# Key projections in a two-layer decoder trunk: the two halves of the memory tokens as one 512-column moving operand, with the two partial sums added by VectorE

## The chip, the cores and the metric

The kernel runs on one core of a Trainium2 chip. The metric is the device time of one execution in microseconds (us). The kernel before takes 1613.98 us, the median of 3 runs (1613.49 to 1614.69).

The engines are named as the profile names them: PE is TensorE's matmul, PEld its weight load, DVE is VectorE, ACT is ScalarE, POOL is GpSimd, SP is SyncE. They run side by side, each through its own list in a fixed order, and wait for each other on semaphores.

## The reference, cut to what matters

Two layers work on 512 tokens of 1024 features. Each has a token mixer, a cross-attention into 256 memory tokens, and an MLP. The change touches the key projection `k = mem @ wk` of the cross-attention, once in each layer:

```python
def _mem_cross_attn(h, mem, wq, wk, wv, wo):
    q = (h @ wq).reshape(bsz, seqlen, XA_HEADS, XA_HEAD_DIM)
    k = (mem @ wk).reshape(bsz, mem.shape[1], XA_HEADS, XA_HEAD_DIM)   # 256 x 1024
    v = (mem @ wv).reshape(bsz, mem.shape[1], XA_HEADS, XA_HEAD_DIM)
    s = jnp.einsum('bthd,bmhd->bhtm', q, k) * (XA_HEAD_DIM ** -0.5)
    pr = jax.nn.softmax(s, axis=-1)
    o = jnp.einsum('bhtm,bmhd->bthd', pr, v).reshape(bsz, seqlen, D_MODEL)
    return o @ wo

for i in range(DEPTH):                      # DEPTH = 2
    ...                                     # h = LN(alpha*h + mixer(h))
    h = _layer_norm(DN_ALPHA * h + _mem_cross_attn(h, mem, ...), ...)
    ffn = jnp.square(jax.nn.relu(h @ ffn_w1[i])) @ ffn_w2[i]
    h = _layer_norm(DN_ALPHA * h + ffn, ...)
```

## The kernel before

**Split numbers.** Every float32 operand of a large matmul is split into a high half (`_hi`, rounded by ACT to the matmul's float32r type) and a low half (`_lo`, what is left, by DVE). A product is the sum of three matmuls: weight high by input high, weight high by input low, weight low by input high.

**Weights** come as a stream of chunks of 128x1024 through three slots. For each chunk SP issues the load of `w_raw`, ACT writes `w_hi` (`split`, L1574), DVE writes `w_lo` (`split`, L2138), and PE reads both. A chunk's slot is free for the chunk three places further on when PE has finished with it (semaphore `chunk_done`). `split(n)` means: all chunks before number n. Keys, values and queries of a layer are 8 chunks each (k_0 to k_7, v_0 to v_7, q_0 to q_7).

**Keys.** `feature_major` (its matmuls are L778) makes one tile of 128 key features by 256 memory tokens from each chunk k_i. For each of the 8 blocks of the contraction it issues the weight's high half against the memory's high half and then against its low half (256 columns each), and after them the weight's low half against the memory's high half, 8 matmuls: 24 matmuls of 256 columns a tile, all summed into columns 0 to 255 of one of the 8 PSUM banks. The memory's halves lie in `aux_hi` and `aux_lo`. ACT then copies the sum from the bank into `k_hi` (`copy_hi`, L1587), and DVE subtracts that from the bank into `k_lo` (L2151).

**What follows on PE.** `to_features` transposes the hidden rows (24 matmuls, L1367) into six banks, which are those of k_0 to k_5; then v_0 is multiplied (L852) into the banks of k_6 and k_7. Each bank is taken when `k_out` says that DVE has written the `k_lo` of the tile in it.

**What sets the order.** Each engine's list is written out by hand. In `attention`, ACT and DVE go through i = 0 to 7, and each i is: `chunk(k_i)`, that is the split of the chunk three places ahead (for i under 3 that is already done in the layer norm before, so that the first one split here is k_5, ahead of tile 3) and then the wait for chunk k_i; then this tile's `k_hi` or `k_lo`. Before tile 0, DVE's list holds the row statistics and the scaling of that layer norm. POOL does nothing in this stretch.

Of the kernel before, what the change touches and what calls it, by code (L numbers as in the profile page):

```python
# [15 lines left out]
F32R = mybir.dt.float32r  # L16
# [212 lines left out]
def build(nc, x_tok, x_feat, mem_feat, weights, vectors, lora, lru_w, ln_rows, out):  # L229
    with ExitStack() as ctx:  # L230
# [3 lines left out]
        def sb(name, shape, dt=F32, at=None):  # L234

            size = 4
            for n in shape[1:]:
                size *= n
            if at is None:
                at = place["at"]  # L240
                place["at"] = at + (size + 31) // 32 * 32
            return nc.alloc_sbuf_tensor_at(name, shape, dt, offset=at)
# [9 lines left out]
        aux_at = place["at"]  # L252
        aux_hi = sb("aux_hi", [P, 8, T], F32R)
        aux_lo = sb("aux_lo", [P, 8, T], F32R)
        b_at = place["at"]
        k_hi = sb("k_hi", [P, 8, MEM], F32R)
        k_lo = sb("k_lo", [P, 8, MEM], F32R)
# [89 lines left out]
        a_hi = sb("a_hi", [P, 2, 4, 256], F32R, at=aux_at + 16384)  # L347
        a_lo = sb("a_lo", [P, 2, 4, 256], F32R, at=aux_at + 24576)
        s3 = sb("s3", [P, 4, 256], at=stage_at + 4 * 2048)

        def a_block(t, k):

# [10 lines left out]
        def hi_slot(c):  # L363
            return w_hi[:, SLOT[c]] if SLOT[c] < W_SLOTS else x_hi[:, SLOT[c] - W_SLOTS]
# [98 lines left out]
        def S(name):  # L463
            if name not in sems:
                sems[name] = ctx.enter_context(nc.semaphore(name))
            return sems[name]
# [5 lines left out]
        def bank(stg, i):  # L472
            return ps[BANK[stg, i]]

        def of(stg, suffix, n):


            return S(FAMILY[stg] + suffix), BEFORE[stg] + n
# [275 lines left out]
        def _(pe):  # L754
# [601 lines left out]
            def to_features(l, which, first=0, last=KD):  # L1356

                n = 3 * l + which
                for t in range(NT):
# [5 lines left out]
                    for k in range(first, last):  # L1365
                        o = take(f"lnt{l}_{which}", k) if t == 0 else bank(f"lnt{l}_{which}", k)
                        ins = pe.transpose(o[:, t * P:t * P + P], h[:, t, k * P:k * P + P], ident[:])  # L1367
                        if t == NT - 1:
                            ins.then_inc(S("lnt_mm"), 1)

            def attention(l):
                pe.wait_ge(S("mem_split"), l + 1)
                memv = [a[:].rearrange("p a t -> p (a t)")[:, 0:8 * MEM].rearrange("p (a t) -> p a t", a=8)
                        for a in (aux_hi, aux_lo)]
                feature_major(f"k{l}", 8, memv[0], memv[1], MEM)
                to_features(l, 0, 0, 6)
                token_major(f"v{l}", 2, KD, memv[0], memv[1], between={4: lambda: to_features(l, 0, 6, 8)})
                def scores(hp, first, last):
# [162 lines left out]
        def _(act):  # L1541
# [17 lines left out]
            def split(upto):  # L1559

                while n_split[0] < min(upto, N_CHUNKS):
                    c = n_split[0]
                    if c not in DOWN_OF:
                        act.wait_ge(landed[RAW[c]], 16 * (NTH_PLAIN[c] // W_SLOTS + 1))
                    else:
                        d, i = DOWN_OF[c]
                        name = PRODUCTS[i // 2][1]
                        if name in B_BLOCK:
                            act.wait_ge(*block_in(name, d))
                        else:  # L1570
                            act.wait_ge(S("t_sum"), 8 * d + 2 * T_ORDER.index(name) + i % 2 + 1)
                    if SLOT_PREV[c] is not None:
                        act.wait_ge(S("chunk_done"), SLOT_PREV[c] + 1)
                    act.activation(hi_slot(c), raw_chunk(c), ACT.Copy).then_inc(S("w_hi_done"), 1)  # L1574
                    n_split[0] += 1
# [10 lines left out]
            def copy_hi(stg, i, dst, n=T):  # L1586
                done(act.activation(dst, bank(stg, i)[:, 0:n], ACT.Copy), FAMILY[stg] + "_hi")  # L1587
# [225 lines left out]

            def memory(l):
                act.wait_ge(S("mem_in"), 16 * (l + 1))
                memv = aux_hi[:].rearrange("p a t -> p (a t)")[:, 0:8 * MEM]
                done(act.activation(memv, stage[:].rearrange("p a t -> p (a t)")[:, 0:8 * MEM], ACT.Copy), "mem_hi")

            def attention(l):
                ln_std(3 * l)  # L1820
                split(FIRST[f"k{l}"] + W_SLOTS)
                for i in range(8):
                    chunk(f"k{l}", i)
                    copy_hi(f"k{l}", i, k_hi[:, i], MEM)
                for half in range(2):
                    for i in range(4):
                        for k in range(4 * half + i + (half + i > 0), min(4 * half + i + 2, KD)):
# [282 lines left out]
        def _(dve):  # L2110
# [12 lines left out]
            def done(ins, name):  # L2123

                counts[name] = counts.get(name, 0) + 1
                ins.then_inc(S(name), 1)
                dve.wait_ge(S(name), counts[name])

            def f(ap):

                return ap.bitcast(F32)
# [9 lines left out]
            def chunk(stg, i):  # L2141
                c = FIRST[stg] + i
                split(c + W_SLOTS)
                dve.wait_ge(S("chunk_done"), c + 1)
# [5 lines left out]
            def tt(o, a, b_, op):  # L2150
                return dve.tensor_tensor(o, a, b_, op)  # L2151
# [376 lines left out]
            def memory(l):  # L2528
                dve.wait_ge(S("mem_hi"), l + 1)
                n8 = 8 * MEM  # L2530
                done(tt(aux_lo[:].rearrange("p a t -> p (a t)")[:, 0:n8], stage[:].rearrange("p a t -> p (a t)")[:, 0:n8],
                        f(aux_hi[:].rearrange("p a t -> p (a t)")[:, 0:n8]), SUB), "mem_split")

            def attention(l):
                split(FIRST[f"k{l}"] + W_SLOTS)
                for i in range(8):
                    chunk(f"k{l}", i)
                    dve.wait_ge(*of(f"k{l}", "_hi", i + 1))
                    done(tt(k_lo[:, i], bank(f"k{l}", i)[:, 0:MEM], f(k_hi[:, i]), SUB), "k_out")
                for half in range(2):  # L2540
                    for i in range(4):
                        for k in range(4 * half + i + (half + i > 0), min(4 * half + i + 2, KD)):
# [446 lines left out]
```

## Time and profile before

| | us |
|---|---|
| median of 3 runs | 1613.98 |
| the profiled execution: its time | 1614.45 |
| its span in the trace | 1612.4 |
| PE busy in it | 1566.9 (97%) |
| DVE busy | 1177.8 (73%) |
| ACT busy | 843.7 (52%) |
| granted TensorE clock, mean | 0.995 |

The span runs from the first to the last instruction in the trace; 2.05 us of the execution's time lie around it. Busy shares are averages over the whole program, and the busy time of PE is that of a pipeline (a matmul's row lasts longer than the distance to the next one), so that what a stretch is limited by is read from its own rows. Layer 1's attention is layer 0's over again, 802.06 us later.

### The profile page before, as it was taken

The numbers are of one execution on the slowest core, as the hardware profiler recorded it, in microseconds if no ns is written. First come the engines' busy times: TensorE is split into PE (matmuls) and PEld (weight loads), VectorE is DVE, ScalarE is ACT, GpSimd is POOL, SyncE is SP. The second block draws the span as 40 slices with busy tenths as digits, with TensorE's granted clock in tenths as the row PEclk, the third lists the DMA queues.
The fourth block names the chain that finished last, engine by engine and source line by source line (L and its number), as shares of the span: only waits on it lengthen the run. The fifth ranks groups of instructions, "written<-read, shape, count | busy, mean of one in ns | idle before, by whom it ended". The sixth has DMA issues, their size and how long they took to land.

```text
span 1612.4 us, 24422 instructions
## 1 busy us (share of the span) xinstructions
PE 1566.9 (97%) x9706; PEld 1303.1 (81%) x9706; DVE 1177.8 (73%) x1356; ACT 843.7 (52%) x1087; POOL 196.7 (12%) x189
## 2 busy tenths in 40 slices
PE   9999999999999999999899989999999999999996
PEld 8877888988878788888687876889887787888885
DVE  4569767664778868686998985756647788676768
ACT  4645643464355454545468855635553654545454
POOL 6111201001100000000026733200010000000001
PEclk9999999999999999999999999999999999999999
DMA  5222004442151505151042220244411605050501
GB/s 214 79 78 67 16 4 146 144 152 70 53 219 43 183 26 178 31 197 38 14 144 79 92 91 14 106 150 138 145 65 53 235 27 186 28 178 27 196 0 52
DMA packets 40784, 159.57 MB, mean 99 GB/s; under 512 B 4064, under 2 KB 4192, under 8 KB 39264
## 3 DMA queue, kind: packets, MB, share of 16 engines
q1 hardware_dynamic: 40384, 155.93, 28.6%
q10 hardware_dynamic: 288, 2.10, 0.3%
q8 instruction: 77, 1.26, 0.3%
q14 instruction: 35, 0.29, 0.1%
HBM read 153.81 MB, written 4.19 MB: 98 GB/s over the span
## 4 chain that ended last, share of the span: by engine, by line
PE 80%; DVE 13%; ACT 4%; issue 3%; POOL 0%; DVEq 0%; ACTq 0%; POOLq 0%
PE bank L778 41%; PE bank L1457 14%; PE bank L852 14%; DVE h L2151 2%; DVE sconv L2154 1%; PE bank L997 1%; PE bank L1012 1%; DVE h L2154 1%; DVE mix L2151 1%; DVE bank L2154 1%; DVE a_lo L2151 1%; DVE lnst L2651 1%; PE bank L1367 1%; DVE w_lo L2138 1%; PE bank L1091 0%
## 5 line engine op out<-in xcount | busy, mean ns | idle before, releaser
L778 PE MATMUL bank<-act_hi,w_hi 128*128 128x512 f32 x840 | 331.7, 396 | 6.0 <-DVE sconv L2154 5.0
L778 PE MATMUL bank<-act_lo,w_hi 128*128 128x512 f32 x840 | 327.4, 391 | 0.0
L2138 DVE TENSOR_TENSOR w_lo<-w_raw,w_hi 128x1024 fp32r<-128x1024 f32 x173 | 218.8, 1270 | 131.4 <-ACT w_hi L1574 128.2
L1574 ACT ACTIVATE w_hi<-w_raw 128x1024 fp32r<-128x1024 f32 x173 | 183.0, 1061 | 111.0 <-PE bank L852 78.2
L778 PE MATMUL bank<-act_hi,w_lo 128*128 128x512 f32 x840 | 212.0, 390 | 0.0
L778 PEld LDWEIGHTS bank<-act_hi,w_hi 128*128 128x128 f32 x840 | 158.6, 189 | 42.7 <-DVE sconv L2154 5.5
L778 PEld LDWEIGHTS bank<-act_lo,w_hi 128*128 128x128 f32 x840 | 158.6, 189 | 34.0 <-issue 1.2
L778 PEld LDWEIGHTS bank<-act_hi,w_lo 128*128 128x128 f32 x840 | 157.9, 188 | 33.0 <-DVE w_lo L2138 0.4
L702 POOL TENSOR_TENSOR cacc<-cacc,cprod 128x512 f32<-128x512 f32 x52 | 75.6, 1454 | 458.3 <-ACT cprod L1944 455.8
L1898 ACT ACTIVATE bank<-bank 128x512 f32<-128x512 f32 x64 | 37.2, 582 | 166.3 <-PE bank L778 166.3
L852 PE MATMUL bank<-w_hi,act_hi 128*128 128x512 f32 x288 | 112.6, 391 | 1.5 <-DVE act_lo L2151 1.5
L852 PE MATMUL bank<-w_hi,act_lo 128*128 128x512 f32 x288 | 112.1, 389 | 0.0
L1889 ACT ACTIVATE a_hi<-a_raw 128x1024 fp32r<-128x1024 f32 x48 | 51.0, 1062 | 67.9 <-PE bank L1457 62.8
L778 PE MATMUL bank<-act_hi,x_hi 128*128 128x512 f32 x208 | 81.5, 392 | 0.7 <-ACT act_hi L1801 0.6
L778 PE MATMUL bank<-act_lo,x_hi 128*128 128x512 f32 x208 | 80.8, 390 | 0.2
L1457 PE MATMUL bank<-w_hi,a_lo 128*128 128x512 f32 x264 | 73.0, 391 | 3.1 <-DVE a_lo L2151 3.0
L852 PE MATMUL bank<-w_lo,act_hi 128*128 128x512 f32 x288 | 74.7, 389 | 0.0
L1457 PE MATMUL bank<-w_hi,a_hi 128*128 128x512 f32 x264 | 72.5, 389 | 0.0
L1457 PE MATMUL bank<-w_lo,a_hi 128*128 128x512 f32 x264 | 71.3, 389 | 0.0
L2151 DVE TENSOR_TENSOR h<-h,bank 128x512 f32<-128x512 f32 x96 | 65.7, 684 | 2.0
L2138 DVE TENSOR_TENSOR w_lo<-b_raw,w_hi 128x1024 fp32r<-128x1024 f32 x46 | 55.4, 1223 | 16.1 <-ACT w_hi L1574 15.2
L852 PEld LDWEIGHTS bank<-w_hi,act_hi 128*128 128x128 f32 x288 | 54.1, 188 | 12.9 <-issue 1.6
(374 smaller groups left out, 3044.2 us busy)
## 6 DMA issues: line engine op xcount, KB each, us to landing
w_raw<-weights SPq DMA_DIRECT2D x199, 512.0 KB, 3.5
b_raw<-weights SPq DMA_DIRECT2D x32, 1024.0 KB, 4.9
gb<-ln_rows SPq DMA_DIRECT2D x6, 1024.0 KB, 8.2
stage<-x_feat SPq DMA_DIRECT2D x4, 512.0 KB, 6.0
h<-x_tok SPq DMA_DIRECT2D x1, 2048.0 KB, 7.9
stage<-mem_feat ACTq DMA_DIRECT2D x2, 1024.0 KB, 7.7
spill<-h SPq DMA_DIRECT2D x1, 2048.0 KB, 6.7
h<-spill SPq DMA_DIRECT2D x1, 2048.0 KB, 7.8
```

Of the source, the lines that this page charges most:

```text
L702: pool.tensor_tensor(cacc2[:, j % 2], cacc2[:, j % 2], cprod[:, added % 2], ALU.add)\
L778: return pe.matmul(banks[i][:, 0:n], w(c0 + i)[:, k * P:k * P + P], x[:, k, 0:n], start=first, stop=last)
L852: return pe.matmul(o[t][:, 0:HALF], x[:, slot[k], t * P:t * P + P], w(c0 + k // 2)[:, kk * HALF:kk * HALF + HALF], start=first, stop=last)
L997: last = each(lambda c, q, tok, feat, cf, ct: pe.matmul(compact(o, j, c, q, n), M_[b][tok, j, ct], halves(NBH[b][tok, j, ct], n, True), st ...
L1012: last = each(lambda c, q, tok, feat, cf, ct: pe.matmul(compact(o, j, c, q, n), left[tok, j, ct], halves(right[tok, j, ct], n, v < 5), sta ...
L1457: return pe.matmul(o[t][:], a[:, slot, k, t * P:t * P + P], w(c0 + k // 2)[:, k % 2 * HALF:k % 2 * HALF + HALF], start=(after is None and ...
L1574: act.activation(hi_slot(c), raw_chunk(c), ACT.Copy).then_inc(S("w_hi_done"), 1)
L1889: done(act.activation(a_hi[:, n % 2], A_OPERAND[name], ACT.Copy), "x_hi")
L1898: step(act.activation(o[:], o[:], ACT.Relu))
L2138: dve.tensor_tensor(lo_slot(c), raw_chunk(c), f(hi_slot(c)), ALU.subtract).then_inc(S("w_split"), 1)
L2151: return dve.tensor_tensor(o, a, b_, op)
L2154: return dve.scalar_tensor_tensor(out=o, in0=a, scalar=s, in1=b_, op0=op0, op1=op1)
```

## The change

The memory's halves lie side by side in one buffer, `mem_both`, in the place where `aux_hi` was. The new `keys` issues for each block one matmul of 512 columns, the weight's high half against both halves of the memory: columns 0 to 255 of the bank get the high part, columns 256 to 511 the low part. The weight's low half goes against the memory's high half as before, into columns 0 to 255. A tile is then 8 matmuls of 512 columns and 8 of 256.

The key is now the sum of the bank's two halves. DVE copies the right half into `k_raw` (a new buffer of two tiles), adds the left half, and raises `t_sum`. ACT, which read the bank, waits for `t_sum` and copies `k_raw` to `k_hi`. DVE then makes `k_lo` out of `k_raw` and `k_hi`. The other users of `t_sum` have their counts moved.

```diff
+        mem_both = sb("mem_both", [P, 2, 8, MEM], F32R, at=aux_at)
+        k_raw = sb("k_raw", [P, 2, MEM], at=stage_at + 4 * 2048)
...
+            def keys(l):
+                for i in range(8):
+                    c = FIRST[f"k{l}"] + i
+                    o = take(f"k{l}", i)
+                    pe.wait_ge(S("w_hi_done"), c + 1)
+                    for k in range(KD):
+                        pe.matmul(o[:], hi_slot(c)[:, k * P:k * P + P], mem_both[:, :, k], start=k == 0, stop=k == KD - 1,
+                                  skip_group_check=True)
+                    pe.wait_ge(S("w_split"), c + 1)
+                    for k in range(KD):
+                        last = pe.matmul(o[:, 0:MEM], lo_slot(c)[:, k * P:k * P + P], mem_both[:, 0, k], start=False,
+                                         stop=k == KD - 1, skip_group_check=True)
+                    last.then_inc(S("chunk_done"), 1)
...
-                feature_major(f"k{l}", 8, memv[0], memv[1], MEM)
+                keys(l)
...   (ACT)
                 for i in range(8):
                     chunk(f"k{l}", i)
-                    copy_hi(f"k{l}", i, k_hi[:, i], MEM)
+                    act.wait_ge(S("t_sum"), key_sum(l, i))
+                    done(act.activation(k_hi[:, i], k_raw[:, i % 2], ACT.Copy), "k_hi")
...   (DVE)
                 for i in range(8):
                     chunk(f"k{l}", i)
+                    step(dve.tensor_copy(k_raw[:, i % 2], bank(f"k{l}", i)[:, MEM:2 * MEM]))
+                    done(tt(k_raw[:, i % 2], k_raw[:, i % 2], bank(f"k{l}", i)[:, 0:MEM], ADD), "t_sum")
                     dve.wait_ge(*of(f"k{l}", "_hi", i + 1))
-                    done(tt(k_lo[:, i], bank(f"k{l}", i)[:, 0:MEM], f(k_hi[:, i]), SUB), "k_out")
+                    done(tt(k_lo[:, i], k_raw[:, i % 2], f(k_hi[:, i]), SUB), "k_out")
```

DVE's list at the start of layer 0's keys, before (bank4 to bank7 and bank0 hold tiles 0 to 4, the first row is the end of the layer norm; line numbers of the two kernels differ):

```order
L2468 TENSOR_SCALAR h_52<-h_52,lnmv_79,lnsd_80 128x1024 [waits dve_step]
L2151 TENSOR_TENSOR k_lo_58<-bank4,k_hi_57 128x256 [waits k_hi,chunk_done,ln_last]
L2151 TENSOR_TENSOR k_lo_58<-bank5,k_hi_57 128x256 [waits k_hi,chunk_done,k_out]
L2151 TENSOR_TENSOR k_lo_58<-bank6,k_hi_57 128x256 [waits k_hi,chunk_done,k_out]
L2138 TENSOR_TENSOR w_lo_51<-w_raw_49,w_hi_50 128x1024 [waits w_hi_done,k_out]
L2151 TENSOR_TENSOR k_lo_58<-bank7,k_hi_57 128x256 [waits k_hi,chunk_done]
L2138 TENSOR_TENSOR w_lo_51<-w_raw_49,w_hi_50 128x1024 [waits w_hi_done,k_out]
```

The same place now:

```order
L2489 TENSOR_SCALAR h_52<-h_52,lnmv_80,lnsd_81 128x1024 [waits dve_step]
L2559 COPY k_raw_103<-bank4 128x256 [waits chunk_done,ln_last]
L2172 TENSOR_TENSOR k_raw_103<-k_raw_103,bank4 128x256 [waits dve_step]
L2172 TENSOR_TENSOR k_lo_59<-k_raw_103,k_hi_58 128x256 [waits k_hi,t_sum]
L2559 COPY k_raw_103<-bank5 128x256 [waits chunk_done,k_out]
L2172 TENSOR_TENSOR k_raw_103<-k_raw_103,bank5 128x256 [waits dve_step]
L2172 TENSOR_TENSOR k_lo_59<-k_raw_103,k_hi_58 128x256 [waits k_hi,t_sum]
L2559 COPY k_raw_103<-bank6 128x256 [waits chunk_done,k_out]
L2172 TENSOR_TENSOR k_raw_103<-k_raw_103,bank6 128x256 [waits dve_step]
L2172 TENSOR_TENSOR k_lo_59<-k_raw_103,k_hi_58 128x256 [waits k_hi,t_sum]
L2159 TENSOR_TENSOR w_lo_51<-w_raw_49,w_hi_50 128x1024 [waits w_hi_done,k_out]
```

Two instructions stand ahead of each `k_lo`, and the `k_lo` stands between them and the next tile's.

ACT's list at the same place, before (the last `w_hi` of the layer norm, tiles 0 to 2, `w_hi` of k_5, tile 3, `w_hi` of k_6):

```order
L1574 ACTIVATE w_hi_50<-w_raw_49 128x1024 [waits chunk_done,w_landed1,ln_std]
L1587 ACTIVATE k_hi_57<-bank4 128x256 [waits chunk_done]
L1587 ACTIVATE k_hi_57<-bank5 128x256 [waits chunk_done,k_hi]
L1587 ACTIVATE k_hi_57<-bank6 128x256 [waits chunk_done,k_hi]
L1574 ACTIVATE w_hi_50<-w_raw_49 128x1024 [waits chunk_done,w_landed2,k_hi]
L1587 ACTIVATE k_hi_57<-bank7 128x256 [waits chunk_done]
L1574 ACTIVATE w_hi_50<-w_raw_49 128x1024 [waits chunk_done,w_landed0,k_hi]
```

And now:

```order
L1594 ACTIVATE w_hi_50<-w_raw_49 128x1024 [waits chunk_done,w_landed1,ln_std]
L1845 ACTIVATE k_hi_58<-k_raw_103 128x256 [waits t_sum,chunk_done]
L1845 ACTIVATE k_hi_58<-k_raw_103 128x256 [waits t_sum,chunk_done,k_hi] x2
L1594 ACTIVATE w_hi_50<-w_raw_49 128x1024 [waits chunk_done,w_landed2,k_hi]
L1845 ACTIVATE k_hi_58<-k_raw_103 128x256 [waits t_sum,chunk_done]
L1594 ACTIVATE w_hi_50<-w_raw_49 128x1024 [waits chunk_done,w_landed0,k_hi]
```

Nothing has moved; each `k_hi` has the wait for `t_sum`, and `w_hi` of the later chunks stands behind it as before.

## Rows read from the trace of the kernel before

**Rows 1.** The page, busy time, share of the span and instructions of each engine.
```profile
PE 1566.9 (97%) x9706; PEld 1303.1 (81%) x9706; DVE 1177.8 (73%) x1356; ACT 843.7 (52%) x1087; POOL 196.7 (12%) x189
```

**Rows 2.** The chain that ended last, in time: start us, us, what.
```profile
297.97 23.03 PE bank L778 x192
321.01 2.62 PE bank L1367 x24
323.63 5.47 PE bank L852 x24
...
1100.03 23.03 PE bank L778 x192
```

**Rows 3.** Timeline of PE, keys to first values: start us, us, engine, line, operation.
```profile
297.81 0.28 PE L778 MATMUL bank<-aux_hi,w_hi 128*128 128x256 f32 x1
...
300.68 0.28 PE L778 MATMUL bank<-aux_hi,w_hi 128*128 128x256 f32 x1
...
320.84 2.78 PE L1367 MATMUL bank<-ident,h 128*128 128x128 f32 x24
323.38 0.47 PE L852 MATMUL bank<-w_hi,aux_hi 128*128 128x512 f32 x1
...
326.21 0.39 PE L852 MATMUL bank<-w_hi,aux_hi 128*128 128x512 f32 x1
...
327.12 0.39 PE L852 MATMUL bank<-w_hi,aux_hi 128*128 128x512 f32 x1
```

**Rows 4.** Timeline of DVE over the keys of layer 0, idle before in brackets.
```profile
307.16 0.81 DVE L2468 TENSOR_SCALAR h<-h,lnmv,lnsd 128x1024 f32<-128x1024 f32 x1
308.01 1.34 DVE L2151 TENSOR_TENSOR k_lo<-bank,k_hi 128x256 fp32r<-128x256 f32 x3
309.38 1.23 DVE L2138 TENSOR_TENSOR w_lo<-w_raw,w_hi 128x1024 fp32r<-128x1024 f32 x1
310.53 0.42 DVE L2151 TENSOR_TENSOR k_lo<-bank,k_hi 128x256 fp32r<-128x256 f32 x1
...
312.89 0.42 DVE L2151 TENSOR_TENSOR k_lo<-bank,k_hi 128x256 fp32r<-128x256 f32 x1 [0.56 <-ACT k_hi L1587]
...
321.53 0.43 DVE L2151 TENSOR_TENSOR k_lo<-bank,k_hi 128x256 fp32r<-128x256 f32 x1 [0.57 <-ACT k_hi L1587]
```

**Rows 5.** Timeline of ACT over the keys of layer 0.
```profile
304.99 0.78 ACT L1587 ACTIVATE k_hi<-bank 128x256 fp32r<-128x256 f32 x2
...
307.12 1.06 ACT L1574 ACTIVATE w_hi<-w_raw 128x1024 fp32r<-128x1024 f32 x1
...
312.40 0.38 ACT L1587 ACTIVATE k_hi<-bank 128x256 fp32r<-128x256 f32 x1 [1.40 <-PE bank L778]
312.82 1.06 ACT L1574 ACTIVATE w_hi<-w_raw 128x1024 fp32r<-128x1024 f32 x1
```

**Rows 6.** Groups of one shape: busy us, mean ns of one | idle before.
```profile
L2468 DVE TENSOR_SCALAR h<-h,lnmv,lnsd 128x1024 f32<-128x1024 f32 x10 | 8.1, 814 | 0.4
L2151 DVE TENSOR_TENSOR k_lo<-bank,k_hi 128x256 fp32r<-128x256 f32 x16 | 6.8, 424 | 4.7 <-ACT k_hi L1587 4.5
L2151 DVE TENSOR_TENSOR v_lo<-bank,v_hi 128x512 fp32r<-128x512 f32 x8 | 5.5, 689 | 1.0 <-ACT v_hi L1587 0.8
L2803 DVE COPY stm<-bank 128x64 f32<-128x64 f32 x2 | 0.4, 224 | 0.1
L2060 ACT ACTIVATE act_hi<-p 128x512 fp32r<-128x512 f32 x8 | 5.1, 632 | 10.5 <-DVE p L2154 10.5
```

**Rows 7.** PE around its longest idle time in this trace.
```profile
932.44 0.80 PE L778 MATMUL bank<-act_hi,w_hi 128*128 128x512 f32 x1 [4.97 <-DVE sconv L2154]
...
936.02 0.40 PE L778 MATMUL bank<-act_hi,w_hi 128*128 128x512 f32 x1
```

**Rows 8.** PE by stretches: length, busy (instructions), granted clock, DMA share, GB/s.
```profile
807.00:808.00 1.00, 1.00 (x4) 0.50 0.72 115
930.00:935.00 5.00, 2.56 (x6) 0.50 0.25 91
```

More of the change, by code:

```diff
@@ L349, in build, with key_sum @@
         s3 = sb("s3", [P, 4, 256], at=stage_at + 4 * 2048)
+        k_raw = sb("k_raw", [P, 2, MEM], at=stage_at + 4 * 2048)
+        def key_sum(l, i):
+            return 8 * (QUARTERS + 1) * l + i + 1
         def a_block(t, k):
@@ L1369, in to_features @@
                             ins.then_inc(S("lnt_mm"), 1)
+            def keys(l):
[11 more added lines that the diff above has]
+                    last.then_inc(S("chunk_done"), 1)
             def attention(l):
                 pe.wait_ge(S("mem_split"), l + 1)
-                memv = [a[:].rearrange("p a t -> p (a t)")[:, 0:8 * MEM].rearrange("p (a t) -> p a t", a=8)
-                        for a in (aux_hi, aux_lo)]
-                feature_major(f"k{l}", 8, memv[0], memv[1], MEM)
+                memv = mem_both[:, 0], mem_both[:, 1]
+                keys(l)
                 to_features(l, 0, 0, 6)
@@ L1570, in split @@
                         else:
-                            act.wait_ge(S("t_sum"), 8 * d + 2 * T_ORDER.index(name) + i % 2 + 1)
+                            act.wait_ge(S("t_sum"), 8 * (d + d // QUARTERS + 1) + 2 * T_ORDER.index(name) + i % 2 + 1)
                     if SLOT_PREV[c] is not None:
@@ L1815, in memory @@
                 act.wait_ge(S("mem_in"), 16 * (l + 1))
-                memv = aux_hi[:].rearrange("p a t -> p (a t)")[:, 0:8 * MEM]
+                memv = mem_both[:, 0].rearrange("p a t -> p (a t)")
                 done(act.activation(memv, stage[:].rearrange("p a t -> p (a t)")[:, 0:8 * MEM], ACT.Copy), "mem_hi")
@@ L2530, in memory @@
                 n8 = 8 * MEM
-                done(tt(aux_lo[:].rearrange("p a t -> p (a t)")[:, 0:n8], stage[:].rearrange("p a t -> p (a t)")[:, 0:n8],
-                        f(aux_hi[:].rearrange("p a t -> p (a t)")[:, 0:n8]), SUB), "mem_split")
+                done(tt(mem_both[:, 1].rearrange("p a t -> p (a t)"), stage[:].rearrange("p a t -> p (a t)")[:, 0:n8],
+                        f(mem_both[:, 0].rearrange("p a t -> p (a t)")), SUB), "mem_split")
             def attention(l):
```

## The prediction

> **What bounds the kernel now.** I read the page first: PE is busy for 97% of the span [rows 1]. Then the chain that ended last, in time: through the keys of each layer it is PE alone, one piece of 23.03 us that ends in the transposes (L1367), and these in the first values (L852) [rows 2]. Then the timelines of this stretch. PE goes from tile to tile without a pause: k_0 begins at 297.81, k_1 at 300.68, so a tile of 24 matmuls takes 2.88 us, 0.120 us for each matmul of 256 columns; the eighth ends at 320.84, the transposes take 2.54 us, and v_0 begins at 323.38 [rows 3]. Layer 1 repeats this 802.06 us later [rows 2].
>
> The share of PE hides how close the other two engines are. Follow one round of theirs: ACT writes `k_hi` from 312.40 to 312.78, then at once `w_hi` of the chunk three places ahead, to 313.88 [rows 5]; DVE takes 0.11 us to see `k_hi` and writes `k_lo` [rows 4], then `w_lo`, whose successor can start 1.15 us after it (309.38 to 310.53) [rows 4]. From the end of a tile that is 0.04 + 0.38 + 0.04 + 1.06 + 0.10 + 1.15 = 2.77 us of a period of 2.88. So they have a tenth of a microsecond to spare per tile, and what keeps PE fed is that they run three chunks ahead. And they start late: DVE is in the layer norm's scaling until 307.97 [rows 4], ACT has its first `k_hi` at 304.99 [rows 5], while k_0 was finished at 300.7.
>
> **The change, part by part.**
>
> PE. Per block of the contraction two matmuls of 256 columns (2 x 0.120 us) become one of 512. The pace of those is in the values: four from 326.21 to 327.12, 0.227 us each [rows 3]. A pair gives back 0.240 - 0.227 = 0.013 us; 64 pairs a layer, 2 layers: 1.7 us. A tile then takes 8 x 0.227 + 8 x 0.120 = 2.77 us. That the 512 columns lie in two pieces I cost at nothing; if it did cost, the sum below would not move, since PE will be the one that waits.
>
> DVE. A copy of 128x256 out of PSUM and an addition are new. The addition is the form of today's `k_lo`, 0.424 us [rows 6]. No copy of this size is in the trace: a copy of 64 elements takes 0.224, and the step from 256 to 512 elements costs a TENSOR_TENSOR 0.265, 1.04 ns an element [rows 6], which puts 256 at 0.224 + 0.200 = 0.424. If a copy ran at half that slope it would be 0.324. I take 0.424, because its source is a bank, and keep 0.324 for the range. For what speaks for the faster one: TENSOR_SCALAR of 1024 elements from SBUF takes 0.814 [rows 6], less than 1024 times 1.04 ns. The Trainium skill ("VectorE: DVE Perf Modes", section "Why PSUM operands drop a tier") says that the double rate for float32 needs a source in SBUF and that a PSUM operand holds the engine at one element a cycle; no row here shows a large plain copy out of PSUM, and by that rule the slower value is the right one.
>
> ACT. `k_hi` now reads SBUF. A copy of 512 from SBUF takes 0.632 [rows 6] and one of 1024 1.06 [rows 5], so 256 takes about 0.42 instead of 0.38.
>
> The new wait. `k_hi` stands behind `t_sum`, and behind `k_hi` in ACT's list stands `w_hi` of the chunk three ahead, without which PE cannot begin that chunk. In DVE's list the next tile's copy stands behind this tile's `k_lo`, which waits for `k_hi`. So nothing of a tile can be worked ahead. Handovers between the engines at 0.10 us, within one at 0.04:
>
> Start. DVE comes to tile 0 at 308.01, as now. A tile of sums costs 0.42 + 0.04 + 0.42 + 0.10 + 0.42 + 0.10 + 0.42 + 0.04 = 1.97 us. Tile 0 is done at 309.98, tile 1 at 311.95, and `k_hi` of tile 2 ends at 313.36. Only then comes `w_hi` of k_5, which stood at 307.12 [rows 5]: it ends at 314.45. PE is ready for k_5 at 297.81 + 5 x 2.77 = 311.67 and waits 2.9 us.
>
> Rounds. Copy 0.42 + 0.04, add 0.42 + 0.10, `k_hi` 0.42 + 0.04, `w_hi` 1.06 + 0.10, `w_lo` 1.15: 3.74 us a tile against PE's 2.77. The loop no longer depends on PE (it needs only chunks that are long done). `k_hi` of tile 3 ends at 317.11 and those after it at 320.85, 324.59, 328.33 and 332.08. PE gets `w_hi` of k_6 at 318.2 and of k_7 at 321.9, waits 1.0 us before each, ends k_7 at 324.8 and the transposes at 327.35.
>
> The banks. v_0 takes the banks of tiles 6 and 7 and needs the last `k_lo`. Today that is written at 321.53 to 321.96, hidden by the transposes [rows 3, 4]. Now it ends at 332.08 + 0.10 + 0.42 = 332.60, and v_0 begins at 332.70 instead of 323.38: 9.3 us later. From there both engines stand to PE as they do now or better, so nothing is lost or won back after it. PE's own gain is in this number already: it is swallowed by the waits.
>
> The clock. PE would stand idle from 327.35 to 332.70, 5.35 us. The longest idle time of before is 4.97 us; after it the granted clock is 0.50, that is 1.2 GHz, and the eight matmuls from 932.44 to 936.02 take 3.58 us instead of 8 x 0.227 = 1.82, a loss of 1.76 us [rows 7, 8]. The only other stretch at 0.50 follows the sparse end of layer 0 [rows 8]. The same fall before v_0 costs about 1.7 us a layer, on the path. A fall at the wait of 2.9 us would cost nothing, since k_6 and k_7 wait for `w_hi` anyway.
>
> Sum: 2 x (9.3 + 1.7) = 22.0 us. The profiled execution took 1614.45, so 1636.4 by it; the median lies 0.5 below it, so 1636.0.
>
> The other hidden costs: loads of `w_raw` follow `w_lo` and land in 3 to 4 us, while each `w_lo` here is followed by the next use of its raw slot more than 7 us later, so they stay hidden. POOL is idle in this stretch.
>
> **Rivals.**
>
> A, the same without the fall of the clock: 2 x 9.3 = 18.6, 1632.6. For it: the idle time is only as long as the one place that shows a fall, and it could come at another phase. Against: that one fell before its idle time was over, and here are three shorter waits just ahead.
>
> B, a faster copy: 0.1 us less in each of 8 rounds, 0.8 us a layer. With the clock's fall 20.3 (1634.3), without it 17.0 (1631.0). The Trainium skill's rule named above speaks against it.
>
> C, `w_hi` alone delays PE and the banks do not (the last `k_lo` is not waited for, or comes early): v_0 begins at 327.35, 4.0 us late, 8 us in all: 1622. The semaphore in PE's list speaks against it.
>
> D, the other side: the change does what it seems to be for. PE's pace remains the bound and 1.7 us are gained: 1612.3, within 0.2% of before. It decides whether DVE and ACT finish a tile within 2.77 us: the round must be 1.0 us shorter than worked out, and the late start must not count. Every term of the round but the copy is read from a row of the same form, and the copy cannot give 1.0. The Trainium skill ("TensorE: Matmul & The Clock Gate", section "Back-to-back issue gap") gives a fixed 2.5 ns per matmul, by which the gain would be 0.3 us instead of 1.7; the rows' 13 ns are the ones that count here, and the sum above holds neither.
>
> E, more than worked out: the low clock lasts longer, or the shifted DVE work meets the queries: over 1640.
>
> **How the numbers follow.** The forecast as worked out 0.62; A 0.17; B 0.07; C 0.05; D 0.03; E 0.06. Least is 1630 (B without the fall is 1631.0, and 0.5 us off a start or handover each way), most 1640 (a copy of 0.5 us and 2.5 us for the clock give 24.8, 1638.8, with a little for E). That holds the forecast, A and B. A difference of 0.2% is 3.2 us, about what a measurement can tell from none: slower 0.96, the same 0.03, faster 0.01.
>
> **What would show it.** Right: DVE's rows over a tile of keys spaced 3.74 us from copy to copy with ACT's `w_hi` in each; PE waiting for ACT `w_hi` before k_5, k_6 and k_7 (2.9, 1.0 and 1.0 us) and 5.3 us for DVE `k_lo` before the first values, with a granted clock of 0.50 behind it; matmuls of 512 columns 0.227 us apart; the copy at 0.424. It would be wrong if the copy took under 0.3, if `w_hi` of k_5 came before `k_hi` of tile 2 was done, or if v_0 did not wait for the last `k_lo`.

## The result, and the profile after

| | before | after |
|---|---|---|
| median, us | 1614.01 (4 runs, 1613.49 to 1614.69) | 1636.72 (4 runs, 1636.19 to 1637.04) |
| the profiled execution, us | 1614.45 | 1636.75 |
| its span, us | 1612.4 | 1635.0 |
| ratio, 95% interval | 1 | 1.0139, 1.0125 to 1.0153 |

The kernel is 22.7 us slower, and PE was given fewer instructions, not more. The page of the kernel after, first busy time, share and instructions of each engine, and further down the chain that ended last, by engine:

```profile
PE 1572.6 (96%) x9578; PEld 1300.0 (80%) x9578; DVE 1190.8 (73%) x1388; ACT 844.7 (52%) x1087; POOL 198.9 (12%) x189
...
PE 78%; DVE 14%; ACT 5%; issue 3%; POOL 0%; DVEq 0%; ACTq 0%; POOLq 0%
```

PE has 128 matmuls fewer than in [rows 1] and DVE 32 instructions more, of 13 us in all. PE's busy time is 5.7 us longer for all that, in part because behind its waits it runs at the lower clock, as shown below. Its share fell by one point only, 97 to 96. What happened in the keys is not to be seen in shares; it is in PE's timeline. Columns: start, us, engine, line, operation, in brackets the idle time before it and what ended it. L1384 are the new matmuls of 512 columns, L1388 those with the weight's low half, L1373 the transposes, L858 the values.

```profile
296.46 1.98 PE L1384 MATMUL bank<-mem_both,w_hi 128*128 128x512 f32 x8
298.27 1.11 PE L1388 MATMUL bank<-mem_both,w_lo 128*128 128x256 f32 x8
299.23 2.00 PE L1384 MATMUL bank<-mem_both,w_hi 128*128 128x512 f32 x8
...
302.02 2.00 PE L1384 MATMUL bank<-mem_both,w_hi 128*128 128x512 f32 x8
...
313.23 3.05 PE L1384 MATMUL bank<-mem_both,w_hi 128*128 128x512 f32 x8 [2.67 <-ACT w_hi L1594]
316.08 1.73 PE L1388 MATMUL bank<-mem_both,w_lo 128*128 128x256 f32 x8
317.65 2.02 PE L1384 MATMUL bank<-mem_both,w_hi 128*128 128x512 f32 x8
...
320.67 2.06 PE L1384 MATMUL bank<-mem_both,w_hi 128*128 128x512 f32 x8
...
323.53 2.78 PE L1373 MATMUL bank<-ident,h 128*128 128x128 f32 x24
331.22 3.60 PE L858 MATMUL bank<-w_hi,mem_both 128*128 128x512 f32 x8 [4.91 <-DVE k_lo L2172]
334.66 1.09 PE L858 MATMUL bank<-w_lo,mem_both 128*128 128x512 f32 x4
```

Against [rows 3]: a tile is 2.77 to 2.79 us long instead of 2.88, as long as PE is fed. At the sixth chunk it is not: 2.67 us of waiting for `w_hi`. The first values wait 4.91 us for the last `k_lo`, where before they followed the transposes at once. From the first key to the first value are 34.76 us instead of 25.57. That the eight matmuls from 331.22 take 3.44 us to the next row is the clock. PE by stretches (length, busy, granted clock, DMA share, GB/s), to be read against [rows 8]:

```profile
328.00:330.00 2.00, 0.00 (x0) 1.00 0.21 84
330.00:332.00 2.00, 0.78 (x2) 0.78 0.72 227
332.00:334.00 2.00, 2.00 (x6) 0.50 0.12 43
334.00:336.00 2.00, 2.00 (x9) 0.87 0.01 4
```

The round behind these waits, in the timeline of DVE and then in that of ACT (the chain that ended last runs through the same instructions, from 310.59 to v_0):

```profile
318.05 0.42 DVE L2559 COPY k_raw<-bank 128x256 f32<-128x256 f32 x1
318.50 0.42 DVE L2172 TENSOR_TENSOR k_raw<-k_raw,bank 128x256 f32<-128x256 f32 x1
319.54 0.43 DVE L2172 TENSOR_TENSOR k_lo<-k_raw,k_hi 128x256 fp32r<-128x256 f32 x1 [0.61 <-ACT k_hi L1845]
320.63 1.22 DVE L2159 TENSOR_TENSOR w_lo<-w_raw,w_hi 128x1024 fp32r<-128x1024 f32 x1 [0.67 <-ACT w_hi L1594]
321.77 0.42 DVE L2559 COPY k_raw<-bank 128x256 f32<-128x256 f32 x1
```

```profile
319.02 0.42 ACT L1845 ACTIVATE k_hi<-k_raw 128x256 fp32r<-128x256 f32 x1 [2.21 <-DVE k_raw L2172]
319.47 1.06 ACT L1594 ACTIVATE w_hi<-w_raw 128x1024 fp32r<-128x1024 f32 x1
322.74 0.42 ACT L1845 ACTIVATE k_hi<-k_raw 128x256 fp32r<-128x256 f32 x1 [2.21 <-DVE k_raw L2172]
```

From copy to copy it is 3.72 us (318.05 to 321.77), and in each of them DVE stands 1.28 us and ACT 2.21 us, in turns, one waiting for the other. Neither is short of time; they are short of work they may do.

Where the 22.6 us of the span come from, by the starts of the first key, the first value and the first query matmul of each layer in the two traces (before: 297.81, 323.38, 346.14; 1099.87, 1125.44, 1148.20; after: 296.46, 331.22, 355.54; 1111.22, 1145.96, 1170.78):

| stretch | before | after | difference |
|---|---|---|---|
| up to k_0 of layer 0 | 297.81 | 296.46 | -1.35 |
| k_0 to v_0, layer 0 | 25.57 | 34.76 | +9.19 |
| v_0 to q_0, layer 0 | 22.76 | 24.32 | +1.56 |
| q_0 to k_0 of layer 1 | 753.73 | 755.68 | +1.95 |
| k_0 to v_0, layer 1 | 25.57 | 34.74 | +9.17 |
| v_0 to q_0, layer 1 | 22.76 | 24.82 | +2.06 |
| the rest | 464.2 | 464.2 | 0 |

21.98 of it lie in the two attentions. The first and the fourth line were in nobody's sum; they nearly cancel here, and a section below comes back to them.

### The profile page after: what moved, and what is told of

Its sections match the earlier page's. It is cut to its first block, busy times and chain, and to the rows that moved or that the text cites. A ratio compares the mean times of both kernels' runs of the same rounds, so it can differ in the third digit from the quotient of the medians.

```text
span 1635.0 us, 24216 instructions
## 1 busy us (share of the span) xinstructions
PE 1572.6 (96%) x9578; PEld 1300.0 (80%) x9578; DVE 1190.8 (73%) x1388; ACT 844.7 (52%) x1087; POOL 198.9 (12%) x189
## 4 chain that ended last, share of the span: by engine, by line
PE 78%; DVE 14%; ACT 5%; issue 3%; POOL 0%; DVEq 0%; ACTq 0%; POOLq 0%
PE bank L784 38%; PE bank L1477 14%; PE bank L858 14%; DVE h L2172 2%; DVE sconv L2175 1%; DVE mix L2172 1%; DVE w_lo L2159 1%; PE bank L1018 1%; PE bank L1003 1%; PE bank L1384 1%; DVE h L2175 1%; ACT w_hi L1594 1%; DVE a_lo L2172 1%; DVE bank L2175 1%; DVE lnst L2674 1%
## 5 line engine op out<-in xcount | busy, mean ns | idle before, releaser
L858 PE MATMUL bank<-w_hi,act_hi 128*128 128x512 f32 x288 | 112.6, 391 | 1.5 <-DVE act_lo L2172 1.5
L858 PE MATMUL bank<-w_hi,act_lo 128*128 128x512 f32 x288 | 112.1, 389 | 0.0
L858 PE MATMUL bank<-w_lo,act_hi 128*128 128x512 f32 x288 | 74.7, 389 | 0.0
L858 PEld LDWEIGHTS bank<-w_hi,act_hi 128*128 128x128 f32 x288 | 54.1, 188 | 12.9 <-issue 1.6
```

Of the source, the lines that this page charges most:

```text
L858: return pe.matmul(o[t][:, 0:HALF], x[:, slot[k], t * P:t * P + P], w(c0 + k // 2)[:, kk * HALF:kk * HALF + HALF], start=first, stop=last)
```

## The experiments

My theory: `k_hi` cannot start before DVE's copy and addition, `w_hi` cannot start before `k_hi`, and the next copy not before `w_lo`, so a tile costs the whole round, and the end of the last round (through the banks) sets v_0; behind the wait the clock falls. The rivals: that PE itself loses by the new matmuls (columns in two pieces, another order), that the added work of DVE and not the waits is what costs, that the clock has no part in it.

**The two halves of the change apart.** First PE's part alone: `keys` as in the change; ACT and DVE as before.

```diff
-                    act.wait_ge(S("t_sum"), key_sum(l, i))
-                    done(act.activation(k_hi[:, i], k_raw[:, i % 2], ACT.Copy), "k_hi")
+                    copy_hi(f"k{l}", i, k_hi[:, i], MEM)
...
-                    step(dve.tensor_copy(k_raw[:, i % 2], bank(f"k{l}", i)[:, MEM:2 * MEM]))
-                    done(tt(k_raw[:, i % 2], k_raw[:, i % 2], bank(f"k{l}", i)[:, 0:MEM], ADD), "t_sum")
                     dve.wait_ge(*of(f"k{l}", "_hi", i + 1))
-                    done(tt(k_lo[:, i], k_raw[:, i % 2], f(k_hi[:, i]), SUB), "k_out")
+                    done(tt(k_lo[:, i], bank(f"k{l}", i)[:, 0:MEM], f(k_hi[:, i]), SUB), "k_out")
```

> PE's part alone: the matmuls of 512 columns as in the changed kernel, while ScalarE and VectorE take the key from the left half of the bank as before. The right half is left out of the sum. Theory (the loss is the round of VectorE and ScalarE, and PE's matmuls are cheaper as worked out): 64 pairs a layer at 0.013 us, 1.7 us less than before, 1612.3, no wait at the keys and none before the first values. Rival (the matmul of 512 columns in two pieces, or the writing of a whole bank, is what costs): slower than before, by up to the 22.7 us. Rival (only 2.5 ns a matmul are fixed): 0.3 us less, 1613.7.

Measured: 1613.02 us (11 runs) against 1614.76 of the kernel before on the same chip, ratio 0.9991 (0.9983 to 1.0000). From k_0 to v_0 are 24.86 us in layer 0 and 24.85 in layer 1, 0.71 less than before, and PE waits for nothing. The end of the keys and the first values:

```profile
318.51 2.78 PE L1373 MATMUL bank<-ident,h 128*128 128x128 f32 x24
321.05 2.08 PE L858 MATMUL bank<-w_hi,mem_both 128*128 128x512 f32 x8
```

So the matmuls do what they are meant to do, about 11 ns for each of the 64 pairs of a layer, and the rival that the new matmuls are what costs is refuted. By the time alone the gain is not settled, since the interval reaches to no change; the profiled execution is one of the slower ones (1614.65 us), with a stretch at the granted clock 0.50 near 1271 us that the profile of before does not have.

Then the other part alone: PE issues before's matmuls of 256 columns, all into the left half. ACT and DVE have the instructions of the change, in number, form and order; since the right half of the bank is unused here, DVE copies the left half and takes the maximum of it with itself, which gives the key again.

```diff
-                        pe.matmul(o[:], hi_slot(c)[:, k * P:k * P + P], mem_both[:, :, k], start=k == 0, stop=k == KD - 1,
-                                  skip_group_check=True)
+                        for m in range(2):
+                            pe.matmul(o[:, 0:MEM], hi_slot(c)[:, k * P:k * P + P], mem_both[:, m, k], start=k == 0 and m == 0,
+                                      stop=False)
...
-                    step(dve.tensor_copy(k_raw[:, i % 2], bank(f"k{l}", i)[:, MEM:2 * MEM]))
-                    done(tt(k_raw[:, i % 2], k_raw[:, i % 2], bank(f"k{l}", i)[:, 0:MEM], ADD), "t_sum")
+                    step(dve.tensor_copy(k_raw[:, i % 2], bank(f"k{l}", i)[:, 0:MEM]))
+                    done(tt(k_raw[:, i % 2], k_raw[:, i % 2], bank(f"k{l}", i)[:, 0:MEM], ALU.max), "t_sum")
```

> The part of VectorE and ScalarE alone: PE has its 24 matmuls of 256 columns as before, all into the left half; VectorE copies the left half, combines it with itself (maximum in place of the sum, same form and size), and the rest is as changed. Theory: the waits swallowed what PE gained, so the first values start at the same time as in the changed kernel: 9.2 us a layer and 1.7 us for the clock, 1636 (within 0.5 us of the changed kernel), waits before k_5, k_6, k_7 of 2.3, 0.9 and 0.9 us. Rival (PE's gain still counts): 1.7 us slower than the changed kernel, 1638.4. Rival (PE's new matmuls cost): near before, 1614 to 1618.

Measured: 1635.89 us (4 runs), ratio 1.0127 (1.0110 to 1.0143), within the interval of the whole change. PE's timeline of this kernel, its rows with a wait in the attention of layer 0:

```profile
314.51 0.71 PE L1385 MATMUL bank<-mem_both,w_hi 128*128 128x256 f32 x4 [2.21 <-ACT w_hi L1595]
...
318.23 2.15 PE L1385 MATMUL bank<-mem_both,w_hi 128*128 128x256 f32 x16 [0.61 <-ACT w_hi L1595]
...
332.50 3.75 PE L858 MATMUL bank<-w_hi,mem_both 128*128 128x512 f32 x8 [4.82 <-DVE k_lo L2173]
```

From k_0 to v_0 are 34.76 us, to the hundredth what the whole change takes, although PE's matmuls need 0.71 us more: its waits are shorter instead (the first by 0.46). In this state of the kernel the matmuls are worth nothing.

**The clock's part.** The whole change, and PE fills the wait before v_0: it writes the last six of the 24 transposes seven times more, 42 in each layer, the same values into the same banks.

```diff
-                        if t == NT - 1:
+                        if t == NT - 1 and (which or first):
                             ins.then_inc(S("lnt_mm"), 1)
+                if which == 0 and first == 0:
+                    for again in range(7):
+                        for k in range(first, last):
+                            ins = pe.transpose(bank(f"lnt{l}_{which}", k)[:, t * P:t * P + P], h[:, t, k * P:k * P + P],
+                                               ident[:])
+                            if again == 6:
+                                ins.then_inc(S("lnt_mm"), 1)
```

> The changed kernel, but PE writes the last six transposes ahead of the first values seven times more (42 transposes of 0.104 us, 4.4 us a layer, same data), in the time in which it stands idle for the last key tile. Theory (1.7 us a layer of the loss is the clock that falls in that idle time): the granted clock stays at 1.0 there, the first values start when they do in the changed kernel and run at full pace: 3.4 us less than the changed kernel, 1633.3. Rival (the clock does not matter, the 9.2 us a layer are more than worked out and something else is late): the same as the changed kernel, 1636.7. Rival (extra work costs): slower.

Measured: 1633.84 us (4 runs), ratio 1.0117 (1.0103 to 1.0131); its span is 1631.6, 3.4 below the kernel after. PE's timeline at v_0, and the stretches there (columns as above):

```profile
326.13 4.75 PE L1379 MATMUL bank<-ident,h 128*128 128x128 f32 x42
331.19 2.08 PE L858 MATMUL bank<-w_hi,mem_both 128*128 128x512 f32 x8 [0.31 <-DVE k_lo L2179]
333.11 1.08 PE L858 MATMUL bank<-w_lo,mem_both 128*128 128x512 f32 x4
```

```profile
328.00:330.00 2.00, 2.00 (x21) 1.00 0.24 98
330.00:332.00 2.00, 1.69 (x13) 1.00 0.69 250
```

v_0 begins where it began after the change (331.19 and 331.22), but its eight matmuls take 1.92 us instead of 3.44, and v_0 to q_0 is 22.77 us again (22.79 in layer 1). The kernel with 84 useless transposes, 42 in each layer, is 2.9 us faster by the medians than the one that leaves PE idle. So the wait sets when v_0 begins, and PE's being idle in it is a second loss, paid behind it.

**One layer alone.** The change in layer 0's keys; layer 1 as before.

```diff
-                keys(l)
+                keys(l) if l == 0 else feature_major(f"k{l}", 8, memv[0], memv[1], MEM)
```

ACT and DVE have the same condition.

> The whole change in layer 0's keys alone, layer 1's as before. My theory: the two layers lose independently of each other, so half of the loss is left: k_0 to v_0 34.76 us in layer 0 (+9.19), v_0 to q_0 24.3 (+1.56), layer 1's 25.57; 11.2 us over before, 1625.5. The rival: a part of the loss comes back later in layer 0 (an MLP or a mixer that waits for loads anyway), so that layer 0 alone costs less than half, under 1624.

Measured: 1626.07 us (4 runs) against 1613.25, ratio 1.0073 (1.0057 to 1.0088), 9.2 to 14.2 us, which takes in the 11.2. k_0 to v_0 is 34.76 us in layer 0 and 25.58 in layer 1. v_0 to q_0 of layer 0 is 25.62 us, 1.3 more than expected, since the low clock lasted longer in this execution:

```profile
334.00:336.00 2.00, 2.00 (x6) 0.50 0.01 4
336.00:338.00 2.00, 2.00 (x8) 0.70 0.84 236
```

The rival, that a part of a layer's loss comes back later, finds nothing in its favour: the first query of layer 1 is 11.43 us later than before (1159.63 against 1148.20).

**The round shortened in two ways.** If the round is the cause, each piece taken out of it must come back. First, ACT copies the right half out of the bank, so that DVE's copy is gone:

```diff
+                    done(act.activation(k_raw[:, i % 2], bank(f"k{l}", i)[:, MEM:2 * MEM], ACT.Copy), "k_right")
                     act.wait_ge(S("t_sum"), key_sum(l, i))
...
-                    step(dve.tensor_copy(k_raw[:, i % 2], bank(f"k{l}", i)[:, MEM:2 * MEM]))
+                    dve.wait_ge(S("k_right"), 8 * l + i + 1)
```

> The changed kernel with one step moved: ScalarE copies the right half of the bank (0.385 us) in place of VectorE, in each tile just before the wait for the sum. The order is otherwise the same. Theory (every term of the round is on the path, and the copy's 0.42 + 0.04 us come off it, since ScalarE does its copy while VectorE makes the low weights): 3.3 us a round instead of 3.7, the first values 5.6 us a layer later than before instead of 9.2, with an idle time of 3.9 us before them; 11.2 us in all, and 3.4 for the clock if it falls there: 1625.2 without, 1628.6 with. Rival (only the wait of PE at k_5 to k_7 counts): 1614 + 2 x 2.5 = 1619. Rival (VectorE's total work counts, not the order): the copy gone is 0.46 x 16 = 7.4 us less than the changed kernel, 1629.3.

Measured: 1629.05 us (4 runs) against 1614.37, ratio 1.0088 (1.0071 to 1.0105). ACT's timeline:

```profile
313.29 0.42 ACT L1846 ACTIVATE k_hi<-k_raw 128x256 fp32r<-128x256 f32 x1 [1.48 <-DVE k_raw L2173]
313.74 1.06 ACT L1594 ACTIVATE w_hi<-w_raw 128x1024 fp32r<-128x1024 f32 x1
314.71 0.36 ACT L1844 ACTIVATE k_raw<-bank 128x256 f32<-128x256 f32 x1
316.55 0.42 ACT L1846 ACTIVATE k_hi<-k_raw 128x256 fp32r<-128x256 f32 x1 [1.48 <-DVE k_raw L2173]
```

The round is 3.26 us (313.29 to 316.55), shorter by the 0.46 of the copy, which ACT does in the shadow of `w_lo`. k_0 to v_0 is 31.03 us, 5.46 over before (5.6 expected), and the wait before v_0 3.51. The rival that only PE's waits at k_5 to k_7 count, 1619, is refuted. The rival that DVE's total work counts and not the order is not: it put the kernel at 1629.3, the theory at 1628.6, and 1629.05 lies between them. The next kernel separates the two, since DVE has the same work in it as in the change.

Second, `w_hi` of the chunk goes ahead of this tile's `k_hi` in ACT's list:

```diff
                 for i in range(8):
                     chunk(f"k{l}", i)
+                    split(FIRST[f"k{l}"] + min(i, 6) + W_SLOTS + 1)
                     act.wait_ge(S("t_sum"), key_sum(l, i))
```

> The changed kernel with one thing moved in ScalarE's list: the high half of the weight chunk three places ahead stands before the high half of this tile's key, so that it no longer waits for the sum. Theory (two things delay PE, the weights and the banks): PE waits less for the weights, but the last low key is still late, since the low key is now no longer hidden behind the high weights: 3.1 us a round, the first values 6.0 us a layer later than before with an idle time of 4.2 us ahead of them, 12.1 us in all, and 3.4 for the clock if it falls: 1626.1 without, 1629.5 with. Rival (the high weights behind the key are the whole loss): near before, 1612 to 1615. Rival (VectorE alone is the bound, order of ScalarE has no effect): 1636.7.

Measured: 1628.43 us (4 runs), ratio 1.0078 (1.0063 to 1.0093). k_0 to v_0 is 31.30 us, 5.73 over before (6.0 expected). ACT's timeline:

```profile
313.78 0.42 ACT L1846 ACTIVATE k_hi<-k_raw 128x256 fp32r<-128x256 f32 x1 [1.51 <-DVE k_raw L2173]
314.23 1.06 ACT L1594 ACTIVATE w_hi<-w_raw 128x1024 fp32r<-128x1024 f32 x1
316.81 0.42 ACT L1846 ACTIVATE k_hi<-k_raw 128x256 fp32r<-128x256 f32 x1 [1.52 <-DVE k_raw L2173]
```

The round is 3.03 us here, 0.69 shorter than in the change. Up to the second `k_hi` nothing is different: it comes 13.16 us behind k_0, in the change 13.15. In both kernels the clock falls as well: v_0 to q_0 is 24.37 and 24.38 us. In this one not an instruction is other than in the change, only their order, and 8 us of the 22 are back, with DVE's work the same. That refutes the rival left over above, and with it the one that ACT's order has no effect (1636.7); the one that `w_hi` behind `k_hi` is the whole loss (1612 to 1615) is refuted as well.

**The round opened.** Both ideas together, and the tiles overlapped: four buffers for the sums instead of two, and the lists of ACT and DVE written out by hand so that each does the next tile's copy or addition while the other works (`r` the copy of the right half, `a` the addition, `h` and `l` the two halves of the key, `w` the split of a chunk; 8 and 9 are the values' first two):

```diff
+        ACT_KEYS = "w5 r0 r1 h0 h1 w6 r2 r3 h2 r4 w7 h3 h4 r5 w8 h5 r6 w9 h6 r7 h7".split()
+        DVE_KEYS = "a0 a1 l0 l1 a2 a3 w5 a4 l2 l3 w6 l4 a5 l5 w7 a6 w8 l6 a7 l7 w9".split()
```

> A version that keeps the new matmuls and takes the round apart: ScalarE copies the right half out of the bank (0.385 us), VectorE only adds and subtracts, there are four tiles of the raw key, and in both lists the steps of up to three tiles are interleaved with the splits, so that no engine waits for the other within one tile. Theory: VectorE has 0.46 + 0.46 + 1.15 = 2.07 us a tile against PE's 2.77, the last low key is written at about the time the transposes end, and the first values start 0.8 us earlier a layer than before: 1612.4, 1.6 us less than before. Rival (any addition on VectorE in this stretch costs, since it starts late): 1 to 3 us more than before. Rival (PE's new matmuls cost): slower by more.

Measured: 1614.77 us (11 runs), ratio 1.0000 (0.9991 to 1.0009). The 22 us are gone, but the expected gain is not there. ACT's timeline, and the row of PE that waits:

```profile
314.75 1.06 ACT L1596 ACTIVATE w_hi<-w_raw 128x1024 fp32r<-128x1024 f32 x1 [1.39 <-DMA w_raw<-weights]
315.71 0.40 ACT L1854 ACTIVATE k_hi<-k_raw 128x256 fp32r<-128x256 f32 x1
```

```profile
317.95 1.22 PE L1390 MATMUL bank<-mem_both,w_lo 128*128 128x256 f32 x8 [0.43 <-DVE w_lo L2168]
```

I had placed `w8`, v_0's chunk, ahead of `h5`. Its raw slot is freed by the `w_lo` of k_5, and the load behind that had not landed: ACT stood 1.39 us with `k_hi` of tile 5 behind it, DVE stood for this `k_hi` with `w_lo` of k_7 behind it, and PE for that. Two exchanges in the lists:

```diff
-        ACT_KEYS = "w5 r0 r1 h0 h1 w6 r2 r3 h2 r4 w7 h3 h4 r5 w8 h5 r6 w9 h6 r7 h7".split()
-        DVE_KEYS = "a0 a1 l0 l1 a2 a3 w5 a4 l2 l3 w6 l4 a5 l5 w7 a6 w8 l6 a7 l7 w9".split()
+        ACT_KEYS = "w5 r0 r1 h0 h1 w6 r2 r3 h2 r4 w7 h3 h4 r5 h5 w8 r6 h6 w9 r7 h7".split()
+        DVE_KEYS = "a0 a1 l0 l1 a2 a3 w5 a4 l2 l3 w6 l4 a5 w7 l5 a6 w8 l6 a7 l7 w9".split()
```

> As the interleaved version before it (ACT copies the right half out of the bank, four buffers for the sums, the work of several tiles interleaved in both lists), with two steps exchanged: in ACT's list the w_hi that waited for its load (v_0's chunk) stands behind k_hi of tile 5, and in DVE's the w_lo of k_7 ahead of the k_lo of tile 5. My theory: PE has no wait from k_0 to v_0, k_0 to v_0 is 24.9 us in each layer instead of 25.55, and the time is that of the kernel with the matmul part alone, 1.4 to 1.7 us less than before, 1613.0. The rival: the lists of ACT and DVE have no room left whatever their order, some other wait of about 0.5 us a layer comes in its place, and the time stays within 0.3 us of before.

Measured: 1611.45 us (11 runs) against 1613.25 (15 runs), ratio 0.9990 (0.9981 to 0.9999), 1.8 us less than before. PE's timeline at the end of the keys has no wait:

```profile
317.98 1.11 PE L1390 MATMUL bank<-mem_both,w_lo 128*128 128x256 f32 x8
318.93 2.78 PE L1375 MATMUL bank<-ident,h 128*128 128x128 f32 x24
321.47 2.08 PE L860 MATMUL bank<-w_hi,mem_both 128*128 128x512 f32 x8
```

k_0 to v_0 is 24.86 us in both layers. So there is room for the added work beside PE, and the arithmetic of the change is kept in full. What was lost was lost by waiting, not by the amount of work. But three things differ from the change here: the copy is on ACT, there are four buffers, and the lists are in another order. The order alone gave 8 us in the kernel with `w_hi` first, and the copy on ACT alone 7.7; whether an order exists that gives back everything with the copy still on DVE was not tried. An estimate from the rows of this kernel says that it would be tight: from its first addition at 306.81 to its last `k_lo` DVE stands idle for 2.6 us, and eight copies are 8 x 0.46 = 3.7. The interval reaches to 0.2 us from no change: that it is faster at all is likely, the size is not settled.

**The kernel before once more,** for what lies outside the attentions.

> The kernel before once more. Nearly all kernels with the new matmuls begin the keys of layer 0 1.4 to 2.1 us earlier than the profile of before does (295.7 to 296.5 instead of 297.8) and win nothing by it by the start of layer 1's keys. If this is a difference from one execution to the next (a load that lands late), this profile shows k_0 near 296.3 or between; if it belongs to the kernel, k_0 stands at 297.8 again and layer 1's at 1099.9. The time is 1614.0 either way.

Measured: 1614.33 us, k_0 at 297.69 and 1099.64, from k_0 to v_0 25.57 and to q_0 another 22.76, as in the first profile. The early k_0 of the others is therefore not a chance of one execution. What is known of it, and where the lead goes, stands under the hardware, below.

## Why the prediction was right, by its own steps

- **PE's gain.** Worked out 13 ns a pair and 1.7 us in all; in the kernel with PE's part alone 11 ns a pair and 0.71 us a layer. The tile is 2.77 us for k_0 and 2.79 for the others. The prediction cited the Trainium skill ("TensorE: Matmul & The Clock Gate", section "Back-to-back issue gap"), whose fixed 2.5 ns for a matmul would have given 0.3 us in all; the Trainium skill gives it there for a matmul by itself. The two layers' keys show 1.4, so the measurement decides for the rows.
- **The copy.** Taken at 0.424, measured at 0.42 in the timeline above. The Trainium skill's rule ("VectorE: DVE Perf Modes", section "Why PSUM operands drop a tier"), that a source in PSUM keeps float32 at the single rate, agrees; rival B had its mechanism in the faster copy and has none.
- **The start.** DVE reached tile 0 at 306.66, not 308.01, because the whole attention lay 1.35 us earlier; counted from k_0 that is 10.20 us, as the prediction had it. A tile of sums cost 1.96 to 1.97 (306.66, 308.62, 310.59), as worked out.
- **The round.** 3.72 instead of 3.74 us. Over five rounds that is 0.1 us, nearly all that is missing there: 9.19 and 9.17 instead of 9.3.
- **PE's waits on the way.** Put at 2.9, 1.0 and 1.0 us, before k_5, k_6 and k_7. The rows of layer 1:

```profile
1127.99 2.08 PE L1384 MATMUL bank<-mem_both,w_hi 128*128 128x512 f32 x8 [2.67 <-ACT w_hi L1594]
...
1131.71 2.08 PE L1384 MATMUL bank<-mem_both,w_hi 128*128 128x512 f32 x8 [0.69 <-ACT w_hi L1594]
...
1135.42 2.09 PE L1384 MATMUL bank<-mem_both,w_hi 128*128 128x512 f32 x8 [0.69 <-ACT w_hi L1594]
...
1145.96 3.75 PE L858 MATMUL bank<-w_hi,mem_both 128*128 128x512 f32 x8 [4.88 <-DVE k_lo L2172]
```

  The brackets say 0.69 where I said 1.0, and half of the difference is in the way of counting: a bracket begins at the end of the last matmul's row, which lies behind the point where the next one could have started (a row of 256 columns is 0.28 us long at a pace of 0.12 [rows 3], so 0.16). The prediction's sum went by the pace: from 1127.99 a tile of 2.77 ends at 1130.76, 0.95 before the next begins. Another 0.1 us is that the first eight matmuls behind a wait take 1.91 us and not 1.82. I should have said which of the two I meant, since I had told readers to look for these numbers in the brackets. In layer 0 there is no wait before k_6 and hardly one before k_7 (0.2 us by the pace): the clock had already fallen at k_5 (its first eight matmuls take 2.85 us), and the slower PE came to k_6 when `w_hi` was there. The prediction's "a fall at the wait of 2.9 us would cost nothing" came true; k_7 begins 24.21 and 24.20 us behind k_0 in the two layers.
- **The banks.** This term decides between 22 us and rival C's 8, and it came as put: PE waits for the last `k_lo` in both layers. By the pace the transposes of layer 0 end at 323.53 + 2.54 = 326.07 and v_0 begins at 331.22, 5.15 us later (4.91 in the bracket) instead of 5.35. Rival C is refuted with it.
- **The clock.** The mechanism was right, the size by chance: 1.56 and 2.06 us in the two layers of the profile after, 1.7 each in the sum, and between 1.4 and 2.9 in nine such places (below). The mechanism is shown by the filled wait, where both are gone and v_0 stays. That kernel, at 1633.84, is close to what rival A described (1632.6), and the kernel after is not that one.
- **Rival D** was right on what PE gains and wrong on whether it counts. Its stated point was a round within 2.77 us; the opened lists get under it and gain 1.8 us.

The prediction's sum, 22.0, is 21.98 in the two attentions. The rest, -1.35 and +1.95, was no part of it, and that they nearly cancel is luck.

## What to carry to other kernels

When a value gets one more step on the way from engine A to engine B, do not ask whether each engine has room for it; follow one round through both lists and see whether the next tile's first step can be done while the other engine works. An in-order list that reads "make, wait, use, next" turns two half-busy engines into one serial chain; here the lists ordered as "make next, use this", with the copy on ACT and two buffers more, gave back the whole loss. And a wait on PE has two prices: the wait, and the matmuls behind it at the lower clock.

## What the runs showed of the hardware

**The clock's price varies with the same wait.** Behind idle times of 3.5 to 4.9 us before v_0, the matmuls from v_0 to q_0 took this much longer than the 22.76 us of before:

| kernel | layer 0, us | layer 1, us |
|---|---|---|
| after | 1.56 | 2.06 |
| one layer alone | 2.86 | |
| vector part | 2.02 | 1.43 |
| ACT's copy | 1.61 | 1.60 |
| `w_hi` first | 1.62 | 1.62 |

The kernel after and the one with one layer alone issue the same instructions up to layer 0's q_0, wait 4.91 us in both, and lose 1.56 and 2.86. So 1.7 us for one fall is good to about a microsecond. Behind 2.67 us of idle time it fell in layer 0 (at k_5) of the kernel after and not in layer 1, where the eight matmuls from 1127.99 take 1.91 us to the next row. The Trainium skill ("TensorE: Matmul & The Clock Gate", section "What's actually happening") says, of the start of a kernel, that the number of matmuls at the lower level varies from run to run of the same kernel; these two executions agree.

**A gain in one place is not kept.** All eight kernels with the new matmuls begin the keys of layer 0 1.2 to 2.1 us before the kernel before, with code ahead of them that computes the same; the one with before's matmuls (the vector part alone) begins at 297.74, like before's two profiles. The lead arises for the most part in a stretch of small matmuls (32 to 128 columns, more than two thousand of them). It begins with a group of 64 columns, at 174.58 us before and at 174.25 after (173.69 to 174.69 in all), and ends at the transposes of `oall`, at 259.66 before and 258.34 after. That is 85.08 us before (85.20 in the second profile, 85.62 in the vector part), 84.09 after, and 83.53 to 84.40 in all eight. The idle rows there name "issue", but their sums do not differ by it (1.6 us before, 1.6 after); what it is stays open.

And in the kernel with PE's part alone, a lead of 2.4 us at 789.67 (before: 792.06) is 0.2 at layer 1's keys. The rows show where it went, in the mixer of layer 1. Before, PE by stretches, the last piece at the low clock and what follows:

```profile
934.00:936.00 2.00, 2.00 (x6) 0.50 0.00 0
936.00:938.00 2.00, 2.00 (x10) 1.00 0.33 66
```

PE's part alone, the waits there and the stretches:

```profile
919.87 0.50 PE L784 MATMUL bank<-act_hi,w_hi 128*128 128x512 f32 x1 [0.82 <-DVE sconv L2174]
...
931.40 0.80 PE L784 MATMUL bank<-act_hi,w_hi 128*128 128x512 f32 x1 [4.51 <-DVE sconv L2174]
```

```profile
934.00:936.00 2.00, 2.00 (x6) 0.50 0.35 68
936.00:938.00 2.00, 2.00 (x8) 0.63 0.49 195
```

PE waits for DVE's `sconv` there, which had not come earlier by as much: of the lead 1.04 are left at 931.40 (before: 932.44). Then the clock, low for longer while PE works, takes 0.8 more. The kernel after has the same pair of waits (0.85 and 4.52), which is a part of its +1.95 there. The opened version kept 2.02 of its lead at the same place (930.42 against 932.44). Why the two differ there was not tried.
